# Reordering VectorE's work at the start of the first MLP: three weight splits ahead of a clear and a bias wait

## The reference

```python
def ada_modulation(c, w, b):
    m = jax.nn.silu(c) @ w + b
    shift, scale, gate = jnp.split(m[:, None, :], 3, axis=-1)
    return shift, scale, 1.0 + gate

def squared_relu_mlp(h, w1, w2):
    return jnp.square(jax.nn.relu(h @ w1)) @ w2

# in each layer of the first block, after the mixer:
        shift, scale, gate = ada_modulation(c, ada_w[layer, 1], ada_b[layer, 1])
        h = x * (1.0 + scale) + shift
        y = squared_relu_mlp(h, mlp_w1[layer], mlp_w2[layer])
        x = layer_norm(DN_ALPHA * x + gate * y, ln_g[layer, 1], ln_b[layer, 1])
```

## Time and profile before

| what | value |
|---|---|
| median of 3 runs | 1420.89 us |
| the runs | 1420.76, 1420.89, 1423.63 us |
| span of the profiled execution | 1418.6 us |
| TensorE busy | 1325.9 us (93%) |
| VectorE busy | 1009.4 us (71%) |
| ScalarE busy | 594.2 us (42%) |
| DMA | 264.18 MB, mean 186 GB/s |
| length of one memset of 128 x 3072 | 2.62 us |
| length of one `low` | 2.28 us |

### The profile page before, as it was taken

The page is one execution under the profiler, slowest core; times in us unless marked ns, Lnnn a source line. Parts: engine busy times, 40 slices in busy tenths (PEclk is TensorE's granted clock), DMA queues, the critical chain, the costliest instruction groups (busy, mean ns, idle before and its releaser), DMA issues.

```text
span 1418.6 us, 20748 instructions
## 1 busy us (share of the span) xinstructions
PE 1325.9 (93%) x7932; PEld 1121.0 (79%) x7932; DVE 1009.4 (71%) x1358; ACT 594.2 (42%) x803; POOL 13.1 (1%) x22
## 2 busy tenths in 40 slices
PE   5986989999999989999989989999999998999997
PEld 1763677888787878888889987888888877888886
DVE  1768488988788878867687884766668665666665
ACT  2543443333344544343354322534337553443432
POOL 0000000000000000000000000000000000000000
PEclk7998999999999998999999999999999999999999
DMA  9753528878367536665535330555554330455540
GB/s 382 284 208 119 179 89 337 322 259 312 131 235 261 166 119 228 248 220 207 197 139 208 123 116 7 206 203 190 195 178 140 111 137 32 167 220 192 200 152 30
DMA packets 45791, 264.18 MB, mean 186 GB/s; under 512 B 5399, under 2 KB 7063, under 8 KB 19994
## 3 DMA queue, kind: packets, MB, share of 16 engines
q1 hardware_dynamic: 32624, 218.19, 42.3%
q10 hardware_dynamic: 13102, 45.09, 9.1%
HBM read 260.89 MB, written 1.05 MB: 185 GB/s over the span
## 4 chain that ended last, share of the span: by engine, by line
PE 80%; DVE 11%; ACT 3%; DMA 3%; issue 2%; SPq 0%; POOL 0%; ACTq 0%; DVEq 0%; POOLq 0%
PE banks L572 16%; PE banks L574 16%; PE banks L573 16%; PE banks L920 14%; PE banks L923 7%; DMA A<-ada_w 3%; PE banks L1215 2%; DVE w_lo L1835 2%; ACT w_hi L1257 1%; PE banks L802 1%; PE banks L749 1%; PE banks L784 1%; PE banks L870 1%; PE banks L815 1%; DVE mx L1946 1%
## 5 line engine op out<-in xcount | busy, mean ns | idle before, releaser
L1835 DVE TENSOR_TENSOR w_lo<-raw,w_hi 128x2048 fp32r<-128x2048 f32 x193 | 439.4, 2286 | 118.1 <-ACT w_hi L1257 115.3
L1257 ACT ACTIVATE w_hi<-raw 128x2048 fp32r<-128x2048 f32 x193 | 368.2, 1914 | 230.9 <-PE banks L574 199.2
L920 PE MATMUL banks<-hT,w_hi 128*128 128x512 f32 x896 | 280.9, 395 | 0.0
L572 PE MATMUL banks<-w_hi,R 128*128 128x512 f32 (+1 forms) x624 | 247.7, 397 | 6.9 <-DVE R L1815 3.4
L573 PE MATMUL banks<-w_lo,R 128*128 128x512 f32 (+1 forms) x624 | 244.2, 391 | 0.0
L574 PE MATMUL banks<-w_hi,R 128*128 128x512 f32 (+1 forms) x624 | 244.1, 391 | 0.0
L923 PEld LDWEIGHTS banks<-hT,w_lo 128*128 128x128 f32 x896 | 168.3, 188 | 39.2
L923 PE MATMUL banks<-hT,w_lo 128*128 128x256 f32 x896 | 176.1, 278 | 0.0
L572 PE MATMUL banks<-hT,w_hi 128*128 128x256 f32 x536 | 158.6, 296 | 8.2 <-DVE hT L2307 6.0
L573 PE MATMUL banks<-hT,w_hi 128*128 128x256 f32 x536 | 154.1, 287 | 0.0
L574 PE MATMUL banks<-hT,w_lo 128*128 128x256 f32 x536 | 154.0, 287 | 0.0
(11 more groups left out here) (266 smaller groups left out, 1487.8 us busy)
## 6 DMA issues: line engine op xcount, KB each, us to landing
raw<-stream SPq DMA_DIRECT2D x193, 1024.0 KB, 4.8
A<-ada_w ACTq DMA_DIRECT2D x73, 512.0 KB, 5.5
A<-ada_w SPq DMA_DIRECT2D x6, 1024.0 KB, 16.8
raw<-ada_w SPq DMA_DIRECT2D x3, 1024.0 KB, 7.6
A<-ln_g ACTq DMA_DIRECT2D x4, 512.0 KB, 3.8
A<-ln_b ACTq DMA_DIRECT2D x4, 512.0 KB, 5.3
A<-ada_w SPq DMA_DIRECT2D x1, 1536.0 KB
A<-A SPq DMA_DIRECT2D x20, 64.0 KB, 4.0
```

The costliest lines, as they stand in the source:

```text
L572: pe.matmul(o, lh, rh, start=start, stop=False, skip_group_check=True)
L920: pe.matmul(two(B[2 * kp + a]), wh[:, kt, P * a:P * a + P], hT[:, :, kt, :], start=kt == 0, stop=False, skip_group_check=True)
L1257: act.activation(w_hi[:, s, :], raw[:, s, :], ACT.Copy).then_inc(hi_done, 1)
L1835: v.tensor_tensor(w_lo[:, s, :], raw[:, s, :], w_hi[:, s, :], ALU.subtract).then_inc(lo_done, 1)
```

## The change

VectorE does its three weight splits first, and clears the sums and waits for their bias behind them. No instruction is added or removed, and the other engines' programs are the same. `s_ada` is set in the first MLP alone, so nothing moves in the other three.

```diff
                 st = n["step"] - 4
+                for u in range(u0, u0 + 3):
+                    low_ahead(u)
                 if s_ada:
                     zero_acc()
                     v.wait_ge(ld_bias, 16 * (s_ada + 1))
-                for u in range(u0, u0 + 3):
-                    low_ahead(u)
                 if s_gate:
                     v.wait_ge(late_bias, 16 * (m + 1))
                     for k in range(2):
```

## The result

The change made the kernel slower: 1428.61 us (median of 4 runs, 1426.39 to 1430.96) against 1420.83 before, a ratio of 1.0061 with a 95% interval of 1.0036 to 1.0085. That is 7.8 us more, where 3.5 were forecast; the time lies 1.1 us above the stated range. A second set gave 1.0063 (1.0036 to 1.0090).

What follows compares the result with a forecast made beforehand. TensorE was taken to bound the kernel, with 80% of the chain. A dn(2) start 1.6 us later, old stall already removed, plus 1.9 us of clock gave +3.5 on 1420.9: 1424.4 us, range 1420.6 to 1427.5.

Steps and rivals of the forecast that it cites:

- the stall at dn(1) goes: TensorE ahead of dn(1): 2.5 us of idle time and 1.9 us of slow clock vanish, 4.4 us off.
- the clear ends 6.6 us later: VectorE: the clear, behind the three splits, ends near 222.1 instead of 215.5, delaying ScalarE's seven DMAs.
- one stall of several us appears ahead of dn(2): TensorE, ready at 229.0, waits 6.0 us for square(2); dn(2) starts at 235.0 instead of 233.40, +1.6 us.
- dn(3) does not stall: TensorE at dn(3): square(3) ends at 245.5, dn(3) wants it at 246.0, a margin of 0.5 us.
- the burst ends again at about 231.0, with the late tile as its last piece: DMA engines: same bytes, always fed, so the late tile lands at 231.0, between bounds of 228.4 and 233.9.
- the late step until square(2) starts 1.2 us: VectorE: from the late tile's landing, the second late step takes 1.2 us until square(2) starts.
- The clock, "I take 1.9": TensorE behind the new stall at dn(2): 1.9 us lost to a lower clock, taken from the old stall.
- The stated upper bound of 2.3: Most the clock could cost behind the dn(2) stall: 2.3 us, from an earlier stretch at 0.50.
- What is issued first is served first: DMA engines: weight units issued ahead of the tiles move first, leaving the late tile as the burst's last piece.
- Rival 1: Late tile lands 9.3 us after issue, at 233.9; dn(2) starts at 238.0, +4.6; 1427.4 to 1427.8 us; chance 0.15.

Runs made afterwards that it cites:

- gate_first: The change, with ScalarE issuing the gate's bias and its two late tiles ahead of the block that waits for the clear; 1423.40 us, ratio 1.0012 to before.
- weights_held: The change, with SyncE loading weight unit 19 and those behind it only once the second late tile has landed; 1427.13 us, ratio 1.0049 to before.
- one_split_held: Against before: one split ahead of the clear, two splits then bias wait behind; SyncE holds unit 20 onward until the second late tile lands; 1424.35 us.
- wait_only: The kernel before with only the bias wait moved behind the three splits, the clear still first; 1426.41 us against 1421.60, ratio 1.0036.

## Why the prediction was wrong

Its sign and its mechanism were right: the stall at dn(1) goes, dn(1) starts at 218.0 at full clock; the clear ends 6.6 us later; square(2) waits for the late tiles behind it; one stall of several us appears ahead of dn(2), released by line 1878; the clock falls behind it; dn(3) does not stall. gate_first confirmed that the late tiles are the cause: with them out of the way 6.2 of 6.8 us went. The sizes failed, each low:

- *"the burst ends again at about 231.0, with the late tile as its last piece"*: this is the step that failed most. The tile landed at 238.75, aligned 233.0: 2.0 us. The end of the burst itself was nearly right; what was wrong is that the tile was taken to be usable when the engines' share falls. The stretches, columns as in the earlier trace rows, of the changed kernel and then of weights_held, in which no weight unit was moving:

```profile
236.00:237.00 1.00, 0.00 (x0) 0.00 (x0) 0.00 (x0) 0.00 (x0) 0.00 (x0) 1.00 1.06 426
237.00:238.00 1.00, 0.00 (x0) 0.00 (x0) 0.25 (x1) 0.00 (x0) 0.00 (x0) 1.00 0.40 160
238.00:239.00 1.00, 0.00 (x0) 0.00 (x0) 1.00 (x1) 0.00 (x0) 0.00 (x0) 0.54 0.02 8
```

```profile
233.00:234.00 1.00, 0.00 (x0) 0.00 (x0) 0.00 (x0) 0.00 (x0) 0.00 (x0) 1.00 1.02 418
234.00:235.00 1.00, 0.00 (x0) 0.00 (x0) 0.20 (x1) 0.00 (x0) 0.00 (x0) 1.00 0.33 131
```

Full rate ends near 237.3 (aligned 231.5) and the tile lands some 1.5 us later; in weights_held it ends near 234.3 and the tile lands at 235.8. The trace of before had it as well: 410 GB/s from 230 to 231, 115 from 231 to 232, and its last weight unit, issued at 224.9, landed 7.9 us later at 232.8. Why the last data are so late is not shown.
- *"the late step until square(2) starts 1.2 us"*: 1.6 us from that landing. The first late step had waited too, for a tile that landed at 237.55, and both steps, 1.28 us each, came behind the wait in one piece, so the second started 0.4 us after its own tile had landed. 0.4 us.
- *The clock, "I take 1.9"*: 2.7 us in this profile by the same reading (2.6 for 1.7 by the timeline), 0.8 more. The stated upper bound of 2.3 was too low as well; one_split_held lost some 3.
- Together 3.5 + 2.0 + 0.4 + 0.8 = 6.7 us, where the stretch has 6.8. The last 1.0 us between the stretch and the 7.8 of the medians lies within the interval of the ratio (5.1 to 12 us). Part of it may be the reference, since the sum took off a fall of the clock that the first profile of before had and the second had not (-1.3 us in the stretch); two profiles do not settle that.

*"What is issued first is served first"* was false: in wait_only the two queues took turns, though four of the five tiles had been issued ahead of the first weight unit. It did little harm here, since in the change the weight units had nearly passed (weights_held: 1 us). Read on into other orders it fails by 5 us and more: by it wait_only had been expected 1 to 2 us faster than before, and it lost 4.0. Rival 1, the tiles as late after their issue as before (9.3 us; it was 8.5), came nearest with 1427.4 to 1427.8, though its reason, a low rate, was not the right one: the engines moved 405 GB/s from 223 to 231 in the changed kernel.

```profile
218.00:223.00 5.00, 5.00 (x30) 4.34 (x29) 5.00 (x3) 1.92 (x1) 0.00 (x0) 1.00 0.69 196
223.00:231.00 8.00, 8.00 (x41) 6.75 (x40) 4.29 (x2) 0.00 (x0) 0.00 (x0) 1.00 0.99 405
231.00:238.00 7.00, 3.97 (x24) 3.29 (x22) 0.25 (x1) 4.20 (x3) 0.00 (x0) 1.00 0.93 372
```

The Trainium skill, DMA: Bandwidth & Descriptors, section "Where 436 GB/s comes from", has such loads bound at about 358 GB/s; the trace of the changed kernel disagrees as that of before did, with these 405.

## What to carry to other kernels

When an instruction moves on one engine, follow what its semaphore releases on the others: here a memset, off the critical path for its own sake, was the gate for seven DMAs, and two steps that wait for them stood in front of the work that TensorE needed. Weigh a load by what is issued beside it as well as by when it is issued; freeing a prefetch earlier takes bandwidth from the load that is urgent. Count a load as usable at its landing, not when the engines' share falls. And send the urgent tile first: reordering ScalarE's issues, with the clear kept early, gained what the change had been able to show at dn(1) and lost at dn(2).

## What was not expected of the hardware

- A DMA issued from SyncE while the engines were full moved nothing for about 3 us (wait_only: issued at 223.3, only the other queue's packets until 226.4), and then had its turn with every packet: 189 to 190 packets, 1.42 to 0.71 MB.
- At the end of a burst the last load landed about 1.5 us after the engines' full rate had ended: 237.3 and 238.75 in the changed kernel, 234.3 and 235.8 in weights_held.
- The same idle stretch of 2.3 us, in two executions of one program, was followed by a granted clock of 0.50 (1.2 GHz) in one and of 1.00 (2.4 GHz) in the other. Behind all seven idle stretches ahead of dn(2), of 2.95 us and more, time was lost to the clock: what the later start of dn(2) leaves of the delay between the 1100th (in dn(0)) and the 1300th matmul, by the timeline's starts, is 2.6 and 2.5 us behind the two of 8.1 us, 2.3 behind 5.5, 2.1 behind 9.2, 1.7 behind 3.0, 1.5 behind 7.2 and 2.9 behind 4.1. The loss does not grow with the idle time.
